# Embedding products kept in PSUM, weight units placed inside VectorE's waits, and a shorter inverse root in a two-layer float32 trunk

## What is computed

```python
def rmsnorm(x, g):
    y = xf * lax.rsqrt(jnp.mean(xf * xf, axis=-1, keepdims=True) + EPS)
    return (y * g).astype(x.dtype)

for i in range(DEPTH):                                    # DEPTH = 2
    x = x + 0.5 * swiglu(rmsnorm(x, ln_ffn1[i]), w_ffn1_gu[i], w_ffn1_down[i])
    h = rmsnorm(x, ln_mix[i])
    x = x + mixer_i(h)                                    # heads, then w_out
    x = x + 0.5 * swiglu(rmsnorm(x, ln_ffn2[i]), w_ffn2_gu[i], w_ffn2_down[i])
    gate = jax.nn.sigmoid(rmsnorm(x, ln_ple[i]) @ w_ple_gate[i])
    x = x + gate * (p[i] @ w_ple_proj[i])                 # p[i] is 256 x 256
return rmsnorm(x, ln_final)
```

## Time and profile before

| | us |
|---|---|
| median of three runs | 1079.36 |
| lowest and highest | 1076.88, 1081.32 |
| the profiled execution | 1079.73 |
| its span (first to last instruction) | 1078.0 |
| PE busy | 1057.0 (98%) |
| PE weight loads busy | 938.1 (87%) |
| DVE busy | 766.1 (71%) |
| ACT busy | 589.5 (55%) |
| POOL busy | 51.4 (5%) |
| mean share of the 16 DMA engines | near 55% |

### The profile page before, as it was taken

One profiled execution on the slowest core, in us unless ns is written; L12 is line 12 of the kernel. 1 busy time (PEld: TensorE's weight loads), 2 busy tenths in 40 slices (PEclk: granted clock), 3 DMA queues, 4 the chain that ended last, 5 costly groups with the idle time before them and its releaser, 6 DMA issues.

```text
span 1078.0 us, 18557 instructions
## 1 busy us (share of the span) xinstructions
PE 1057.0 (98%) x6712; PEld 938.1 (87%) x6712; DVE 766.1 (71%) x1378; ACT 589.5 (55%) x1010; POOL 51.4 (5%) x100
## 2 busy tenths in 40 slices
PE   9999999999999999999999999999999999999996
PEld 8888888999879888888988888889998888888886
DVE  5978765666546977755699787656767797876566
ACT  6756544435546655543565655455565665654453
POOL 1000001000002000000020000010000200000100
PEclk9999999999999999999999999999999999999999
DMA  8765447574322755456647664468633376544731
GB/s 276 254 197 173 136 140 211 178 216 135 118 79 89 235 195 195 124 145 189 205 157 235 195 195 146 133 189 273 210 109 119 110 259 195 168 141 141 212 131 40
DMA packets 226008, 184.47 MB, mean 171 GB/s; under 512 B 4680, under 2 KB 224544, under 8 KB 225952
## 3 DMA queue, kind: packets, MB, share of 16 engines
q1 hardware_dynamic: 222288, 180.90, 53.7%
q10 hardware_dynamic: 3664, 2.85, 0.9%
HBM read 182.54 MB, written 1.06 MB: 170 GB/s over the span
## 4 chain that ended last, share of the span: by engine, by line
PE 90%; DVE 5%; issue 2%; ACT 1%; DMA 1%; POOL 0%; DVEq 0%; SPq 0%; POOLq 0%; ACTq 0%
PE ps L1235 44%; PE ps L1236 22%; PE ps L1226 4%; PE ps L1227 4%; PE ps L1228 4%; DVE wsp L825 2%; PE ps L1350 2%; PE ps L1351 2%; PE ps L1352 2%; PE ps L1455 1%; PE ps L1442 1%; PE ps L1484 1%; DMA raw<-in_w_ffn_gu_dram 1%; PE ps L1461 0%; ACT wsp L533 0%
## 5 line engine op out<-in xcount | busy, mean ns | idle before, releaser
L825 DVE TENSOR_TENSOR wsp<-raw,wsp 128x1024 fp32r<-128x1024 f32 (+1 forms) x382 | 417.5, 1110 | 61.6 <-ACT wsp L533 60.5
L1235 PE MATMUL ps<-xsA,wsp 128*128 128x512 f32 x1056 | 375.1, 400 | 1.6 <-DVE wsp L825 1.0
L533 ACT ACTIVATE wsp<-raw 128x1024 fp32r<-128x1024 f32 (+1 forms) x382 | 355.8, 958 | 25.2 <-PE ps L1228 20.5
L1236 PE MATMUL ps<-xsA,wsp 128*128 128x256 f32 x1056 | 296.5, 281 | 0.0
L1235 PE MATMUL ps<-hff,wsp 128*128 128x512 f32 x704 | 247.8, 397 | 0.0
L1235 PEld LDWEIGHTS ps<-xsA,wsp 128*128 128x128 f32 x1056 | 198.4, 188 | 52.9 <-issue 1.8
L1236 PEld LDWEIGHTS ps<-xsA,wsp 128*128 128x128 f32 x1056 | 199.5, 189 | 0.0
L1236 PE MATMUL ps<-hff,wsp 128*128 128x256 f32 x704 | 197.6, 281 | 0.0
L1235 PEld LDWEIGHTS ps<-hff,wsp 128*128 128x128 f32 x704 | 132.1, 188 | 32.0
L1236 PEld LDWEIGHTS ps<-hff,wsp 128*128 128x128 f32 x704 | 133.0, 189 | 0.0
L1235 PE MATMUL ps<-xsB,wsp 128*128 128x512 f32 x352 | 123.0, 393 | 3.4 <-DVE xsB L887 1.8
(11 more groups left out here) (201 smaller groups left out, 1319.8 us busy)
## 6 DMA issues: line engine op xcount, KB each, us to landing
raw<-in_w_ffn_gu_dram SPq DMA_DIRECT2D x87, 1024.0 KB, 5.1
raw<-in_w_ffn_down_dram SPq DMA_DIRECT2D x64, 704.0 KB, 4.7
raw<-in_w_in_even_dram SPq DMA_DIRECT2D x12, 1024.0 KB, 5.9
raw<-in_w_in_odd_dram SPq DMA_DIRECT2D x9, 1024.0 KB, 6.0
raw<-in_w_ple_gate_dram SPq DMA_DIRECT2D x8, 1024.0 KB, 6.0
raw<-in_w_out_even_dram SPq DMA_DIRECT2D x4, 1024.0 KB, 5.1
raw<-in_w_out_odd_dram SPq DMA_DIRECT2D x4, 1024.0 KB, 6.0
raw<-in_w_ple_proj_dram SPq DMA_DIRECT2D x2, 1024.0 KB, 5.0
```

Of the source, the lines that this page charges most:

```text
L533: act.activation(wsp[:, s, 0, half * n:(half + 1) * n], raw[:, s, half * n:(half + 1) * n], ACT.Copy).then_inc(hi, 1)
L825: dve.tensor_tensor(wsp[:, s, 1, sl], raw[:, s, sl], wsp[:, s, 0, sl].bitcast(F32), ALU.subtract).then_inc(lo, 1)
L1235: pe.matmul(ps[:, bank, :], whi, moving.rearrange("p s t -> p (s t)"), start=first, stop=False)
L1236: return pe.matmul(ps[:, bank, SEQ:], wlo, moving[:, 0, :], start=False, stop=last)
```

## The change

**Layer 0's embedding products stay in PSUM.** Two `p` tiles share a bank (banks 2 to 5). ACT's eight copies into `proj` are gone, and so are its and DVE's waits for the `p` tiles; DVE multiplies the sigmoid by the tile in PSUM. The gate tiles use banks 0, 1, 7, 6 in turn instead of 0 to 3. Banks 7 and 6 are those of the column sums and the row, so the third gate tile waits for `rstd`.

**Units.** In both embedding gates one unit stands ahead of the root on DVE. In layer 0 two units stand between `rdiag` and the wait for the row; four units instead of none stand ahead of ACT's table load. In layer 1 three units instead of two follow the root. In front of three of the four feed-forwards (norms 2, 4 and 6) one unit moves from behind the wait for the row to ahead of it.

**Root.** A Newton turn is three instructions on both columns, each with a wait for the one before, where it was four instructions on one column each with two waits.

The diff, cut to its core:

```diff
 def ple_bank(kind, m):
-    return m % 4 if kind == "g" else (m + 4) % 6
+    return (0, 1, 7, 6)[m % 4] if kind == "g" else 2 + m // 2
+def ple_cols(kind, m):
+    return slice(m % 2 * SEQ, (m % 2 + 1) * SEQ) if kind == "p" else slice(0, SEQ)

-        PLE_UNITS = {"p": (0, 1, 0, 1, 0, 1, 0, 0), "g": (1, 1, 1, 1, 1, 1, 1, 0)}
+        GATE_UNITS = (1, 1, 1, 1, 1, 1, 0, 0)

 # ACT, ple
-                advance(2 * (ph_proj.c0 + 2))
+                advance(2 * (ph_proj.c0 + 4))
                 nc.scalar.preload_act_table_set("sigmoid_and_others")
-                    if kind == "p":
-                        act.activation(proj[:, m], ps[:, ple_bank(kind, m), 0:SEQ], ACT.Copy).then_inc(proj_ready, 1)
 # ACT, ple_rows
-                advance(2 * (ph_proj.c0 + 2))
-                nc.scalar.preload_act_table_set("sigmoid_and_others")
+                advance(2 * (ph_proj.c0 + 2) + 1)
-                    advance(ptr[0] + (0, 1, 1, 0)[i])
+                    advance(ptr[0] + (0, 1, 0, 2)[i])
+                nc.scalar.preload_act_table_set("sigmoid_and_others")

 # DVE, inverse_root(norm, ahead=0)
-                    square_term(0)
-                    step(square_term(1))
-                    corrected(0)
-                    last = corrected(1)
+                    step(dve.tensor_tensor(rtmp[:], rcol[:], rcol[:], ALU.mult))
+                    step(dve.tensor_tensor(rtmp[:], rtmp[:], nhalf[:], ALU.mult))
+                    last = dve.scalar_tensor_tensor(rcol[:], rtmp[:], 1.5, rcol[:], ALU.add, ALU.mult)
+                advance(ptr[0] + ahead)
                 dve.wait_ge(row_done, norm + 1)

 # DVE, ple
-                advance(2 * (ph_proj.c0 + 2))
+                advance(2 * (ph_proj.c0 + 2) + 1)
+                inverse_root(norm - 1, ahead=2)
+                advance(2 * (ph_proj.c0 + 4))
-                        dve.wait_ge(proj_ready, KD * layer + m + 1)
-                        dve.tensor_tensor(silu[:], silu[:], proj[:, m], ALU.mult).then_inc(g_prod, 1)
+                    dve.tensor_tensor(silu[:], silu[:], ps[:, ple_bank("p", m), ple_cols("p", m)], ALU.mult).then_inc(g_prod, 1)
 # DVE, ple_rows
-                advance(2 * (ph_proj.c0 + 2))
+                advance(2 * (ph_proj.c0 + 2) + 1)
                 inverse_root(7)
-                advance(2 * (ph_proj.c0 + 3))
+                advance(2 * (ph_proj.c0 + 4))
 # DVE, before gate_up
-                        inverse_root(norm - 1)
+                        inverse_root(norm - 1, ahead=1)

 # PE, ple
-                    reuse(bank)
+                    if kind == "g" or m % 2 == 0:
+                        reuse(bank)
-                    reader[bank] = (proj_ready if kind == "p" else g_norm, KD * ph_proj.layer + m + 1)
+                    reader[bank] = (g_prod if kind == "p" else g_norm, KD * ph_proj.layer + (m | (kind == "p")) + 1)
                     if (kind, m) == ("g", 0):
                         spread_rows(norm)
+                        for b in (BANK_COL, BANK_ROW):
+                            reader[b] = (rstd_ready, norm + 1)
```

61 lines of the change are left out of this document (24 added, 37 removed).

## The result

The changed kernel took **1067.92 us** (median of 6 runs, 1064.78 to 1070.09) against 1078.77 us for the kernel before on the same chip (6 runs, 1076.25 to 1081.32): ratio 0.9905, 95% interval 0.9879 to 0.9930. That is 10.85 us less; 7.4 us were forecast, and 1067.92 lies outside the range of 1070.0 to 1075.8. The profiled execution of after took 1064.78 us, its span is 1063.1 us, 14.9 us shorter than before's 1078.0. (Three disturbed executions of the later series are left out of every time given here: one of 2039 us in `root_only`, which was its profiled one, one of 1722 us in `after_third`, and one of 1145 us of the kernel before.)

What follows compares the result with a forecast made beforehand. PE, busy 98% of the span, bounds the kernel, so only its waits can be won. Terms 0.55 + 3.95 + 0.7 + 2.2 = 7.4 us, taken from the median 1079.36, gave 1072.0 us, range 1070.0 to 1075.8.

Steps and rivals of the forecast that it cites:

- the signs of its being wrong: Third gate tile waiting for `rstd`; DVE idle for ACT's half; diagonals late at start; layer 1 third/fourth gate tile wait.
- runs' own spread: Rival: PE stalls turn up elsewhere, or the runs' 2 us spread around the median hides a part; about 1076 us, chance 0.10.
- the ceiling: Most the change could win: PE's marked waits at its places, 7.2 us, plus unmarked short holds, 8.1 us in all.
- Start: Program start: the shorter first root covers PE's wait for the diagonals, -0.55 us.
- Layer 0's gate and the feed-forward of norm 4: Units moved ahead start gate tiles 2.3 us earlier; low-part wait goes, 0.5 us remains at norm 4's loop; -3.95 us.
- Norms 2 and 6: Feed-forwards of these norms: one unit moves into idle time ahead of the row, ending PE's 0.36 us waits; -0.7 us together.
- Layer 1's gate: Layer 1's embedding gate: three units behind the root come in time, both PE waits go, -2.2 us.
- The root: DVE's inverse root: new turn 0.63 us instead of 0.86, 0.7 us saved a root, on the path only at the start.
- The rival of a root that isn't shorter: Rival: new root instructions take 0.30 us each, so the root saves nothing; about 1073.0 us, chance 0.15.
- The products in PSUM: Layer 0's gate: removing ACT's copies is worth nothing by itself; DVE's multiply costs the same from PSUM.
- ACT in layer 1: Rival: ACT's units or table load run late in layer 1's gate, most of 2.2 us stays; 1074.2 us, chance 0.10.
- the row in layer 0: Rival: ACT's half comes late, delaying `rstd` and the third gate tile; slower beyond 9.6 us lateness, chance 0.03.

Runs made afterwards that it cites:

- root_only: The kernel before with the new three-instruction Newton turn in all roots, nothing else changed: 1075.66 us, ratio 0.9962 to before.
- after_third: The changed kernel, unedited, run again on another chip: 1068.47 us, ratio 0.9960 to before.
- the alternated pair: Both kernels with the 512- and 256-column matmuls swapped in every second step: before 1073.42 us, changed 1064.96 us on one chip.
- after_oldroot0: The changed kernel with the old Newton turn in the first root alone: 1068.72 us, ratio 0.9915 to before.
- after_copies: The changed kernel with ACT copying layer 0's embedding products to SBUF again, two tiles at a time: 1070.03 us, ratio 0.9945 to before.
- before_again: The kernel before, unedited, run and profiled once more: 1079.37 us, ratio 0.9998 to before.

## Why the prediction was wrong, point by point

**Sign and mechanisms held.** What would show it right came out, but for the root, which is 2.43 us long where 2.5 to 2.6 was said: no wait for a low part of `xsB` and none in layer 1, one wait for a unit of 0.44 us at the loop of norm 4 (0.3 to 0.5), tile work 1.60 us behind `rstd` (1.6), multiply by PSUM 0.41 us. None of the signs of its being wrong is in the profile.

**The step that failed is the last one, from the sum to the runs.** The prediction set its sum against one profiled execution and a median of three, took their distance of 0.4 us for all the uncertainty there was, and drew the lower end of the range from "every wait goes, and the median is a little low". It has no term for time that PE loses while busy, and the page before could not show one, since PE is drawn as busy at either pace. In fact an execution carries 0 to 4 slow stretches of 3.4 us. The forecast of 1072.0 was 4.1 us too high. The medians of all runs split this. 2.0 us of it is the starting point: 1079.36 was taken, and the 140 undisturbed runs of before, over several chips, have 1077.3. Another 1.7 us is the distance between the kernels, 9.1 us by all runs where 7.4 was forecast. The last 0.4 us is the luck of after's first six runs, 1067.92 against 1068.3 for all 21. So 1.8 to 2.4 of the 10.85 us measured are chance, and without that chance the time would still have come out under 1070.0, since the starting point was too high and the gain too small. What would have warned: three runs that differ by 4.4 us in the table of the times before, on a kernel without another disturbance, and a third stretch with more matmuls in 70 us than the three others. The rival "runs' own spread" looked for it on one side only.

**The sum was too small by 0.6 to 1.1 us**: 7.4 forecast, 8.0 by places, and 8.46 (7.9 to 9.2) by the alternated pair, which is above what the prediction called the ceiling (8.1).
- *Start*, 0.55 forecast, 0.68 measured across the row spread (0.5 by `after_oldroot0`). The wait for the diagonals went as said; a matmul behind a wait is drawn 0.50 us long and its successor starts 0.31 to 0.34 us later instead of 0.24, so every wait that goes gives 0.1 us more than idle time + 0.16.
- *Layer 0's gate and the feed-forward of norm 4*, 3.95 forecast, 4.0 measured (0.31 + 3.70). By parts: 2.5 for layer 0's gate alone, 1.1 for the unit ahead of the row alone, the rest only with both.
- *Norms 2 and 6*, 0.36 forecast for each, 0.48 measured, the same 0.1 for the restart.
- *Layer 1's gate*, 2.2 forecast, 2.4 measured: two restarts. Nothing was given back at the end, as said.

**The root.** 0.7 us saved forecast from 0.21 us an instruction, 0.82 measured: nine instructions 0.195 us apart, a turn of 0.59 us instead of 0.86. DVE's groups of after, 518 to 568 us (count | busy us, mean ns | idle):

```profile
L1107 DVE TENSOR_TENSOR silu<-silu,ps 128x256 f32<-128x256 f32 x8 | 3.3, 411 | 1.1 <-ACT silu L753 1.1
...
L910 DVE TENSOR_TENSOR rtmp<-rcol 128x2 f32<-128x2 f32 x6 | 1.0, 161 | 0.2
```

An instruction on two columns without a per-partition operand takes 161 ns; the old ones with two such operands took 269 and 209. The rival of a root that isn't shorter falls.

**The products in PSUM.** The multiply with a PSUM operand takes 411 ns, the one from SBUF took 416. The Trainium skill ("VectorE: DVE Perf Modes", the section on the TRN2 errata) has a higher cost for a PSUM source, 0.065 us more by the prediction's estimate from its cycles; for this instruction the trace doesn't show it (in `after_copies`, with the operand in SBUF, it takes 415 ns), and the measurement decides. That the edit is worth nothing by itself was forecast, and `after_copies` shows 0.3 us.

**ACT in layer 1, and the row in layer 0.** ACT's table load ends at 1033.64 and its first sigmoid starts at 1034.46, when PE's tile is there. The units ahead of `rstd` end 0.40 us before the row arrives, and no wait of PE for `rstd` is listed. Both rivals fall.

**What stays open.** What it is in a wait or a row spread that makes one pace or the other follow, and why the slow one repeats every three steps, no run here shows. Why the clock falls in the mixer of layer 0, or behind the wait of norm 4, in some executions only stays open as well. How many slow stretches a timed run carried is estimated from its time, not seen: only profiled executions show their paces.

## What to carry over

When the engine that bounds a kernel is "100% busy", count its instructions in equal windows of equal work before and after: a busy share hides a pace, and here chance in the pace (0 to 13.5 us) can be larger than the edit (8 us). Where runs of one kernel spread more than their waits explain, compare two kernels by the distance between matmuls whose work is the same, or first take the spread away (here by the order of the matmuls) and measure then. And weight units, or any work of which an amount is due by some time, belong into the idle time that an engine has ahead of a fixed arrival: here two units ahead of the row cost nothing (DVE still idled 0.40 us), and behind it they delayed the tile's work by 2.3 us.

## What the runs showed of the chip

- **Two paces of one instruction stream.** Alternating float32 matmuls of 512 and 256 columns run at 0.3467 or at 0.3533 us a pair, both at a granted clock of 1.00, and keep the pace until PE next waits or spreads a row (15 of 24 added waits were followed by the slow one; at 13 of 18 row spreads without idle time the pace changed). In the order 512, 256, 256, 512 there is one pace, 0.3483.
- **A short wait can cost the clock.** Behind the wait of 1.8 us for a low part, one and the same kernel kept its clock in one execution and had a mean of 0.66 and 0.92 for 4 us each in another, 1.7 us worth of matmuls. The stretch as a whole is 1.1 us longer by it, because short holds for late units fall away meanwhile. Windows over it, of before and of `before_again` (columns as above):

```profile
560.00:564.00 4.00, 3.33 (x17) 1.00 0.11 39
```

```profile
560.00:564.00 4.00, 3.68 (x14) 0.66 0.06 19
564.00:568.00 4.00, 4.00 (x24) 0.92 0.40 123
```

- **A one-column matmul in a run of wide ones costs 0.22 us** (two instructions in the profile), two thirds of a step that has 768 columns.
- **A VectorE operation on SBUF operands can take twice as long beside GpSimd.** The add to `xT` of the gate tiles of after takes 0.42 us at 531.67, with GpSimd idle, and 0.83 at 536.61, where GpSimd's own add runs from 536.41 for 0.74 us.
